# Experts' results weighted on the way out of PSUM and summed by an accumulating scatter

## What is computed

```python
# block one
for e in range(16):
    h = silu(t @ w_e_gate[e]) * (t @ w_e_up[e])
    y = y + comb[:, e:e + 1] * (h @ w_e_down[e])      # comb: routing weight, 0 where not chosen
# block two, rows sorted by expert into blocks of 128
gu = xe @ w_gu[e] + b_gu[e]
act = (clip(gu[:, D_FF:]) + 1) * (x_glu * sigmoid(1.702 * x_glu))   # x_glu = min(gu[:, :D_FF], 7)
yb = act @ w_dn[e] + b_dn[e]
y = zeros((T + 1, D)).at[slot_tok].add(yb * slot_w[:, None])
x = x + gt2 * rmsnorm(y[:T], g_post_ffn)
```

## Time and profile before

| | us |
|---|---|
| median of 3 runs (2850.87 to 2857.93) | 2851.93 |
| profiled execution, its own time | 2854.47 |
| its span, first to last instruction | 2852.7 |
| PE busy | 2502.2 (88%) |
| DVE busy | 2201.2 (77%) |
| ACT busy | 1598.9 (56%) |
| POOL busy | 370.3 (13%) |
| moved by DMA | 731.58 MB, mean 256 GB/s |
| mean granted TensorE clock | 0.934 |

### The profile page before, as it was taken

One profiled execution on the slowest core, in us unless ns is written; L12 is line 12 of the kernel. 1 busy time (PEld: TensorE's weight loads), 2 busy tenths in 40 slices (PEclk: granted clock), 3 DMA queues, 4 the chain that ended last, 5 costly groups with the idle time before them and its releaser, 6 DMA issues. The chain is left out here.

```text
span 2852.7 us, 35466 instructions
## 1 busy us (share of the span) xinstructions
PE 2502.2 (88%) x11972; PEld 2024.1 (71%) x11972; DVE 2201.2 (77%) x2167; ACT 1598.9 (56%) x1491; POOL 370.3 (13%) x297
## 2 busy tenths in 40 slices
PE   7987776999939997778948999999999999999992
PEld 6844665777728895767746777777777777877772
DVE  6787766899854405877557888899988989989985
ACT  3215625777744314555215667677766767667762
POOL 1212001333200000000001111111111111111210
PEclk9998977999969998989958999999999999999996
DMA  8765217999942410021236999999999999999995
GB/s 323 257 214 164 53 55 277 397 400 400 377 143 93 129 53 1 1 89 45 84 126 234 359 363 356 356 360 363 365 365 362 363 362 365 365 356 362 367 353 200
DMA packets 248415, 731.58 MB, mean 256 GB/s; under 512 B 29948, under 2 KB 57867, under 8 KB 246095
## 3 DMA queue, kind: packets, MB, share of 16 engines
q1 hardware_dynamic: 222132, 639.35, 62.2%
q0 software_dynamic: 22240, 80.75, 7.5%
q10 hardware_dynamic: 3968, 10.49, 1.0%
HBM read 692.73 MB, written 39.39 MB: 257 GB/s over the span
## 5 line engine op out<-in xcount | busy, mean ns | idle before, releaser
L49 PE MATMUL psum_all<-sb_ring_r,sb_arena_r 128*128 128x512 f32 (+1 forms) x2400 | 924.7, 385 | 0.0
L157 DVE TENSOR_TENSOR sb_ring_r<-sb_ring,sb_hi_ring 128x2048 fp32r<-128x2048 f32 x285 | 648.7, 2287 | 202.5 <-ACT sb_hi_ring L148 196.1
L148 ACT ACTIVATE sb_hi_ring<-sb_ring 128x2048 fp32r<-128x2048 f32 x285 | 543.3, 1914 | 191.5 <-DMA sb_ring<-in_w_dn_dram 54.1
L157 DVE TENSOR_TENSOR sb_ring_r<-sb_ring,sb_arena_r 128x2048 fp32r<-128x2048 f32 x258 | 581.8, 2284 | 41.2 <-ACT sb_arena_r L148 39.6
L148 ACT ACTIVATE sb_arena_r<-sb_ring 128x2048 fp32r<-128x2048 f32 x258 | 484.5, 1911 | 212.0 <-DMA sb_ring<-in_w_gu_dram 200.3
L48 PE MATMUL psum_all<-sb_hi_ring,sb_arena_r 128*128 128x512 f32 (+1 forms) x1352 | 513.0, 379 | 15.0 <-DVE sb_ring_r L157 5.2
L49 PEld LDWEIGHTS psum_all<-sb_ring_r,sb_arena_r 128*128 128x128 f32 x2400 | 459.1, 191 | 91.8
L50 PE MATMUL psum_all<-sb_hi_ring,sb_arena_r 128*128 128x512 f32 (+1 forms) x1352 | 508.6, 376 | 0.0
L48 PE MATMUL psum_all<-sb_arena_r 128*128 128x512 f32 x1064 | 429.4, 404 | 6.7 <-DVE sb_arena_r L2224 4.7
L50 PE MATMUL psum_all<-sb_arena_r 128*128 128x512 f32 x1080 | 428.0, 396 | 0.0
L48 PEld LDWEIGHTS psum_all<-sb_hi_ring,sb_arena_r 128*128 128x128 f32 x1352 | 259.0, 192 | 68.3 <-DVE sb_ring_r L157 9.5
(11 more groups left out here) (459 smaller groups left out, 3078.5 us busy)
## 6 DMA issues: line engine op xcount, KB each, us to landing
sb_ring<-in_w_gu_dram SPq DMA_DIRECT2D x272, 1024.0 KB, 6.8
sb_ring<-in_w_dn_dram SPq DMA_DIRECT2D x136, 1024.0 KB, 9.3
sb_ring<-in_w_e_gate_dram SPq DMA_DIRECT2D x36, 1024.0 KB, 9.3
sb_ring<-in_w_e_up_dram SPq DMA_DIRECT2D x36, 1024.0 KB, 10.3
sb_ring<-in_w_e_down_dram SPq DMA_DIRECT2D x36, 1024.0 KB, 9.0
sb_ring<-in_w_in_dram SPq DMA_DIRECT2D x27, 1024.0 KB, 5.8
sb_arena<-in_w_ada_dram POOLq DMA_DIRECT2D x32, 512.0 KB, 5.8
sb_ring<-in_w_mod_dram SPq DMA_DIRECT2D x16, 1024.0 KB, 5.2
```

What stands on the lines that cost most here:

```text
L49: eng.matmul(out, a[0], b[1], start=False, stop=False)
L148: act.activation(s.hi[c % len(s.hi)], s.raw[c % len(s.raw)], ACT.Copy).then_inc(s.hi_made, 1)
L157: dve.tensor_tensor(s.lo[c % len(s.lo)], s.raw[c % len(s.raw)], s.hi[c % len(s.hi)].bitcast(F32), ALU.subtract).then_inc(s.lo_made, 1)
```

## The change

One row of y per token. Before the loop y is preset: in block one to zeros, which `route` stores; in block two to routing weights times down biases, which the start of `experts` computes: `route` sums the chosen one-hots times weights into `k.comb` (tokens x experts), TensorE turns it, and eight plain fp32 matmuls with the 32 rows of the down biases give four tiles, which ScalarE copies out of PSUM and SyncE stores. `route` also lists each slot's weight (`item_hot` becomes twice as wide) into `R.share`. `put_y` multiplies by it, and the scatter adds in DRAM. The down projection's bias matmuls, their `select`, and half of the bias table are gone. The combines load one row per token and neither weigh nor add.

```diff
@@ route, SyncE
+            if m.bias is None:
+                sp.wait_ge(s.zeroed, 1)
+                for t in range(TT):
+                    sp.dma_start(m.y[t * P:(t + 1) * P, :], zero).then_inc(R.y_ready, 16)
+            else:
+                b_up, b_down = m.bias
+                sp.dma_start(k.pair[0:m.experts]..., b_down).then_inc(R.bias_landed, 16)
+                sp.wait_ge(s.logits, 1)
+                for half in range(2):
+                    sp.dma_start(k.rows[32 * half:32 * half + m.experts]..., b_up).then_inc(R.bias_landed, 16)
@@ route, POOL
+            if m.bias is None:
+                pool.memset(zero, 0.0).then_inc(s.zeroed, 1)
+            else:
+                pool.wait_ge(s.weighed, 1)
+                for r in range(top):
+                    pool.tensor_tensor(shares[r], chosen[:, r], wide(R.weight[:, :, r], 2, E), ALU.mult)...
+                for r in range(1, top):
+                    pool.tensor_tensor(k.comb[:] if r == top - 1 else shares[0], shares[0], shares[r], ALU.add)...
@@ route, TensorE and VectorE
-                ins = pe.matmul(k.psum[:, 3, 0:NI], slot_hot[:, i, :], item_hot[:, i, :], ...)
+                ins = pe.matmul(k.psum[:, 3, 0:2 * NI], slot_hot[:, i, :], item_hot[:, i, :], ...)
                     dve.tensor_scalar(slot_hot[:, pair, :], k.iota[:], slot_f[:, t, r:r + 1], None, ALU.is_equal)
-                    dve.tensor_scalar(item_hot[:, pair, :], ..., place[:, t, r:r + 1], ...)
+                    dve.tensor_scalar(item_hot[:, pair, 0:NI], ..., place[:, t:t + 1], ...)
+                    dve.tensor_scalar(item_hot[:, pair, NI:2 * NI], ..., R.weight[:, t, r:r + 1], ...)
+            link(dve.tensor_copy(R.share[:, 0:NI], k.psum[:, 3, NI:2 * NI]))
@@ experts, SyncE, after the first item's chunks
+            if biased:
+                for t in range(TT):
+                    sp.wait_ge(s.y_made, t + 1)
+                    sp.dma_start(m.y[t * P:(t + 1) * P, :], first_y[t]).then_inc(R.y_ready, 16)
@@ experts, POOL
                 pool.indirect_dma_start(m.y, bass.IndirectOffsetOnAxis(ap=to_row.bitcast(U32), axis=0),
-                                        ysb.rearrange("p h n -> p (h n)"), None).then_inc(s.y_stored, 16)
+                                        ysb.rearrange("p h n -> p (h n)"), None, compute_op=ALU.add
+                                        ).then_inc(s.y_stored, 16)
             gather(0, True)
             gather(1)
+            pool.wait_ge(R.y_ready, 16 * TT)
@@ experts, TensorE, down()
                         pe.wait_ge(s.y_put, j + 1)
-                        if biased:
-                            pe.wait_ge(s.sel_down, jj)
-                            for hf in range(2):
-                                pe.matmul(k.psum[:, YB + hf, :], sel_down, bias_hl[...], start=True, stop=False)
@@ experts, TensorE, before the first item
+            if biased:
+                for t in range(TT):
+                    ins = pe.transpose(k.psum[0:m.experts, YB, t * P:(t + 1) * P], k.comb[:, t, :], k.ident[:])
+                ins.then_inc(s.comb_turned, 1)
+                pe.wait_ge(s.comb_read, 1)
+                pe.wait_ge(R.bias_landed, 48)
+                for t in range(TT):
+                    if t == 3:
+                        pe.wait_ge(s.y_made, 1)
+                    for hf in range(2):
+                        ins = pe.matmul(k.psum[:, 2 * (t % 3) + hf, :], comb_t[:, t * P:(t + 1) * P],
+                                        b_down[:, 512 * hf:512 * hf + 512], start=True, stop=True)
+                    ins.then_inc(s.y_summed, 1)
             turn_x(0, True)
+            if biased:
+                pe.wait_ge(s.y_made, TT)
@@ experts, ScalarE
                 act.activation(ysb..., k.psum[:, YB:YB + 2, :]...,
-                               ACT.Copy).then_inc(s.y_put, 1)
+                               ACT.Copy, scale=R.share[:, bass.ds(j, 1)]).then_inc(s.y_put, 1)
+            if biased:
+                act.wait_ge(s.comb_turned, 1)
+                act.activation(comb_t, k.psum[0:m.experts, YB, :], ACT.Copy).then_inc(s.comb_read, 1)
             make_hi(act, k, ss, 0)
+            if biased:
+                for t in range(TT):
+                    act.wait_ge(s.y_summed, t + 1)
+                    act.activation(first_y[t], k.psum[:, 2 * (t % 3):2 * (t % 3) + 2, :]..., ACT.Copy).then_inc(s.y_made, 1)
@@ experts, VectorE, before the loop over items
+            if biased:
+                dve.wait_ge(R.y_ready, 16 * TT)
@@ combine_and_normalise and combine_and_store
-            for r in range(2):
-                sp.dma_start(got[:, 2 * t + r, :], y[r * T + t * P:r * T + (t + 1) * P, :])...
+            sp.dma_start(got[:, t, :], y[t * P:(t + 1) * P, :]).then_inc(landed_y[t], 16)
-            act.activation(got[:, 2 * t, :], got[:, 2 * t, :], ACT.Copy, scale=R.weight[:, t, 0:1])...
-            link(dve.scalar_tensor_tensor(out=other, in0=other, scalar=R.weight[:, t, 1:2], in1=mine, ...))
@@ combine_and_store, one transfer, no weighing, no adds
-                ins = dve.scalar_tensor_tensor(out=total[:, t, :], in0=got[:, top * t + r, :],
-                                               scalar=R.weight[:, t, r:r + 1], in1=total[:, t, :], ...)
```

More of the change, by code:

```diff
@@ L1727, in route @@
         pos_i, slot_i, item_i, slot_f, item_f = (take(TT, top) for _ in range(5))
-        place, dest, empty = take(TT, top), take(NI), take(NI)
-        slot_hot, item_hot = take(TT * top, P), take(TT * top, NI)
+        place, dest, empty = take(TT), take(NI), take(NI)
+        shares = [take(TT, E) for _ in range(top)]
+        slot_hot, item_hot = take(TT * top, P), take(TT * top, 2 * NI)
         if G:
@@ L1782, in _ @@
             link(dve.tensor_tensor(logits, psum, wide(bias, 1, TT), ALU.add))
+            dve.sem_inc(s.logits, 1)
             if G:
@@ L1844, in _ @@
             link(dve.tensor_copy(item_f, item_i.bitcast(I32)))
-            for r in range(top):
-                ins = dve.tensor_scalar(place[:, :, r], k.token[:], 1.0 + r * T, None, ALU.add)
-            link(ins)
+            link(dve.tensor_scalar(place, k.token[:], 1.0, None, ALU.add))
             for t in range(TT):
@@ L1925, in experts @@
     if biased:
[L1926 to L1929, removed]
+        bias_hl = take(m.bias[0].shape[1], True)
+        bias_raw = k.rows[0:64].rearrange("p a d -> p (a d)")
+        sel_up = [take(P, True) for _ in range(2)]
+        b_down, comb_t = k.pair[0:m.experts].rearrange("p a d -> p (a d)"), take(T)[0:m.experts]
+        first_y = [prod, h, take(D), take(D)]
     more_hi = [take(CHUNK, True) for _ in range(SLOTS - HI_SLOTS)]
@@ L1958, in _ @@
         def _(sp):
-            if biased:
-                for half in range(2):
-                    for b, raw in zip(m.bias, bias_raw):
-                        sp.dma_start(raw[32 * half:32 * half + b.shape[0], :], b).then_inc(s.bias, 16)
             def up(e, part, c0, per, j):
@@ L2320, in _ @@
                 silu_up(n - 1, PER * n - nB)
-            if biased:
-                select(sel_down, n - 1, s.sel_down)
             done = min(nB, HI_SLOTS)
@@ L2513, in vector @@
         link = chain(dve, s.chain)
-        def add(t):
-            dve.wait_ge(s.weighted, t + 1)
-            for r in range(1, top):
-                dve.wait_ge(landed_y[top * t + r], 16)
-                ins = dve.scalar_tensor_tensor(out=total[:, t, :], in0=got[:, top * t + r, :], scalar=R.weight[:, t, r:r + 1],
-                                               in1=total[:, t, :], op0=ALU.mult, op1=ALU.add)
-                if r < top - 1:
-                    link(ins)
-            ins.then_inc(s.summed, 1)
         def mean(t):
```

135 lines of the change are left out of this document (60 added, 75 removed).

## The result

| | before | after |
|---|---|---|
| median, 6 runs each on one chip | 2853.19 (2848.51 to 2857.93) | 2864.53 (2858.49 to 2866.72) |
| profiled execution, its span | 2852.7 | 2863.7 |
| mean granted TensorE clock | 0.934 | 0.935 |

The changed kernel takes 1.0038 times the time of the one before, 95% interval 1.0026 to 1.0051: 11 us slower, where +31 was forecast. One execution each of x6_sums_moved (7732 us) and x10_no_gate_product_after (7422 us), at a granted clock of 1.00, is left out of their ratios; nothing on record explains them. The scatter is now line L2048, the output copy L2209, the hidden half L2276, the up bias L2101.

A forecast was written before the change was run, and what follows sets the result against it. The prediction took the first loop as DMA-bound with TensorE level, and some 24 of 34 second-loop items as without slack. Its terms, +22 + 25 + 1.3 + 1.3 - 16 - 6.4 + 1.8 + 1 + 1 = +31, gave 2883 us, range 2817 to 2960.

The forecast's parts named there:

- d: Both loops: DMA-engine time of one accumulating scatter above a plain one, taken as 1.3 us, bounds 0 and 3.4.
- +22: First loop: 17 scatters at 1.3 us more each, with no spare DMA time, add 22 us.
- the free add: Rival, both loops: the scatter's addition costs no DMA time, 2818 us in all; chance 0.20.
- the serial trip: Rival, both loops: adding costs a further serial trip, 3.4 us a scatter, 2991 us; chance 0.22 (or between).
- In 24 items: 24 x (1.3 - 0.47) = +20 us.: Second loop: 24 items without slack pay 1.3 us for the scatter, less 0.47 for the removed bias matmuls.
- the forecast's own sign: Both loops: the prediction is wrong if the periods do not grow, or grow by more than 2 us.
- The minus: Second loop: the removed pair of bias matmuls, with its wait, saves 0.47 us per item.
- The plus: Second loop: the scatter's added 1.3 us stands ahead of the first down chunk, in full where no slack is left.
- the second loop swallows it: Rival: the add costs 1.3 us but is covered in the second loop, 2842 us; chance 0.16.
- the 24 waits: Second loop: TensorE waited 24 times, 17.1 us in all, at the first down matmul, just behind the scatter.
- the -15.5 for the biases: Second loop: removing the bias matmuls saves 33 x 0.47 = 15.5 us, a term the rivals booked too.
- -16 + 1.3: Behind block two's last scatter: the one-row combine saves 16 us, the lone scatter costs 1.3 more.

The follow-up runs named there:

- x6_sums_moved: Changed kernel with the bias sums moved behind the chunks of the first item's gate projection; 2860.96 us, ratio to before 1.0026.
- x10_no_gate_product_after: Changed kernel without VectorE's product of gate and sigmoid in block two (wrong activation there); 2853.84 us, ratio to before 1.0004.
- the mean of the six: Mean second-loop stage of six profiles, the changed kernel's among them, that run the same code in its steady state: 1239.4 us (1236.4 to 1243.5).
- x3_no_down_bias: Kernel before without the two down-bias matmuls, their wait and their select, scatter still plain; 2847.9 us, ratio to before 0.9974.
- x2_bias_back: Changed kernel with two bias-like matmuls put back ahead of each block-two down projection, on other operands; 2877.01 us, ratio to before 1.0069.
- x9_no_gate_product: Kernel before without VectorE's product of gate and sigmoid in block two (wrong activation there); 2849.5 us, ratio to before 0.9987.
- x11_after_and_plain: Changed kernel with a second, plain scatter of the same rows into another DRAM tensor behind each accumulating one; 2948.23 us, ratio to before 1.0337.
- x4: Kernel before with every scatter issued a second time, plain, into another DRAM tensor; 2893.45 us, ratio to before 1.0124.
- x7: Changed kernel with block one as before the change, so the change is in block two alone; 2843.54 us, ratio to before 0.9965.
- x5: Changed kernel with its eight bias-sum matmuls over 128 rows, 96 of them zeros; 2854.81 us, ratio to before 1.0005.
- x1: Changed kernel with a plain, overwriting scatter, so a token's rows are not summed; 2836.31 us, ratio to before 0.9929.
- x12: x7 with its eight bias-sum matmuls over 128 rows, 96 of them zeros; 2836.8 us, ratio to before 0.9951.

## Why the prediction was right or wrong

**Right: the price of the add and the first loop.** d = 1.3 was forecast, 1.28 measured there; the software queue's share 19.5% where about 21% was to show it (that had counted 13.6 MB as before, but slower periods hold fewer transfers); the period 19.63 us against the forecast 19.6; the stage +19.7 against +22. The two rivals about d, the free add (0 us) and the serial trip (3.4 us), fall by the same rows.

**Wrong: the second loop.** The step that failed is "In 24 items: 24 x (1.3 - 0.47) = +20 us. In the other 9 that have a scatter ahead I take 0.3 us of slack: 9 x 0.5 = +5. Together +25 us." The measured stage is -2.2, or +0.2 by the mean of the six. By the forecast's own sign, a loop whose period does not grow, this part is wrong: 37.62 before, 37.63 after. The wait at the first down matmul, which was to grow to 1.5 us in nearly all items, is 24.1 us in 31, 0.8 each. Both terms in the bracket were mis-taken. Mean durations of TensorE's segments between 1700 and 2600 us, per item, show it; the nominal chunk is 2.80:

| us per item | last gate chunk, with wait for the hidden half | bias pair | down 1 | down 2 | down 3 | down 4 | period |
|---|---|---|---|---|---|---|---|
| before | 3.64 | 0.54 | 2.80 | 2.80 | 2.83 | 2.82 | 37.66 |
| x3_no_down_bias | 3.47 | - | 2.86 | 2.93 | 3.18 | 2.89 | 37.51 |
| x2_bias_back | 4.20 | 0.54 | 2.80 | 2.80 | 2.80 | 2.80 | 38.09 |
| after | 3.88 | - | 2.87 | 2.80 | 3.03 | 2.90 | 37.64 |
| x9_no_gate_product | 3.53 | 0.54 | 2.80 | 2.80 | 2.82 | 2.81 | 37.52 |
| x10_no_gate_product_after | 3.93 | - | 2.87 | 2.80 | 2.80 | 2.81 | 37.36 |
| x11_after_and_plain | 5.13 | - | 3.67 | 2.80 | 2.90 | 2.85 | 39.65 |

*The minus did not come.* The 0.54 us (taken at 0.47) that TensorE no longer spends on biases come back as waits in the down chunks: from before to x3, +0.06, +0.13, +0.35 and +0.07, 0.61 together. One item of the changed kernel, its scatter in the timeline and then its chain of waits, for the earlier trace rows:

```profile
2236.98 2.90 POOL L2048 DMA_INDIRECT y_dram<-sb_arena  x1 [24.74 <-ACT sb_arena L2209]
...
2242.61 10.37 DMA sb_ring<-in_w_dn_dram
...
2253.09 1.93 ACT sb_hi_ring L148
...
2255.03 2.29 DVE sb_ring_r L157
...
2257.33 0.59 DVE sb_arena_r L2276
...
2258.38 1.83 DVE sb_ring_r L157
...
2260.58 1.22 DVE sb_arena L2281
...
2261.79 1.18 DVE sb_ring_r L157
...
2263.91 0.87 DVE sb_arena L2286
...
2265.05 2.29 DVE sb_ring_r L157
```

Before, the chain went from the hidden half (1.15) to TensorE. Now it stays on VectorE for seven instructions, 10.3 us of work in 12.3 us, splits of weights with the gate's clip (L2281) and its product with the sigmoid (L2286) between them, before it returns to TensorE. Behind the down chunk's landing two paths of nearly equal length run side by side: TensorE's bias pair and four chunks (11.8 us before), and VectorE's work for the same chunks. Shortening TensorE's alone left VectorE's. The forecast had asked of the loop what TensorE and the DMA engines had left, and not VectorE (busy for 994.76 of 1100 us), and had priced the bias pair from TensorE's row alone. VectorE's path was so near that 0.1 us an item (3.2 us in 33) was all that its turn left of the saving, and TensorE's waits of before show almost nothing of it (3.2 us in 900).

*The plus did not come either.* I had taken an item without slack to pass on all of d. With d in place the wait for the hidden half grew by 0.56 an item (x2) or 0.24 (after), not 1.3 to 1.5. The landings point to where the rest went. The scatter's own, before:

```profile
y_dram<-sb_arena POOLq DMA_INDIRECT x29, 8.3
```

It went from 8.3 to 10.6 us, the down chunk's from 9.4 to 9.7, and for the scatter's nobody waits in a hurry. The loop's 362 GB/s against 399 did mean room, though the DMA share stood at 0.99: x4 moved 372 GB/s there. The argument against the rival "the second loop swallows it" was the 24 waits; that rival had the d part nearly right, and its 2842 missed because it too booked the -15.5 for the biases. x11 shows that the room was good for about one scatter's worth: the next 1.3 us arrived in full.

Set against its own twin without the add, each kernel's wait grew by about as much: 0.41 us from x3 to the changed kernel, 0.56 from the kernel before to x2. But in the changed kernel part of this falls where TensorE would have waited for VectorE a little later: down 2 and down 3 are 0.13 and 0.15 shorter than in x3, and the period grew by 0.13 only. This may be why the add costs 14.5 us with the bias pair and next to nothing without it; it is read from the table and was not tested by itself. What holds the shift at 0.4 to 0.6 out of 1.3 to 1.5 us is open. That the transfers share the engines, so that a longer one mostly delays itself, fits the landings but was not tested by itself either.

**The small terms.** Behind the last scatter: forecast -16 + 1.3, measured -13.5. Its chain, for the earlier trace rows:

```profile
2835.76 6.28 DMA y_dram<-sb_arena
...
2842.47 4.60 DMA sb_arena<-y_dram
...
2849.80 1.29 DVE sb_arena L2544
...
2859.18 0.69 DVE sb_x L2548
```

The scatter takes 6.28 us instead of 3.38 when it stands alone: +2.9, where I had put d, 1.3. Beside other traffic d is engine time, alone it is latency, and that is twice as much. The same fits block one's last scatter: from it to the next stage's first matmul 42.9 us before, 38.95 after, so -4.0 against -6.4 + 1.3. Route of block two: from that matmul to the last instruction +7.8 in this profile, +3.6, +4.0 and +4.3 in x7, x5 and x1, against +3.4 worked out; the rest is this profile's own. I had let the loop's start absorb it. It did not, because the bias sums took 14.0 us, the upper bound, where I took 10: from routing's last instruction to the first up matmul 23.0 us (22.2 before, forecast 19 to 23), and to the first scatter 86.0 (86.2 before). With the -4.0 and the +7.8 these make up "between", +3.6 against -3.1. The first stage's +3.4 against +1.8 lies within what it varies from run to run (478.8 to 486.4).

Summed by the measured stages: +3.4 + 19.7 + 3.6 - 2.2 - 13.5 = +11.0, the difference of the spans.

## What to carry to other kernels

An addition in DRAM costs a second transfer's DMA time; put it in the loop whose bytes per second lie below what the same engines reach elsewhere in the trace, and not in the one at that rate (here: block two alone, 0.9965 instead of 1.0038). Before booking a saving on the bound engine, measure the other engine's path between the same two events, since a path 0.1 us shorter hardly shows in the waits; and do not add up two such edits, because the four corners of a square can be 1239, 1236, 1254 and, with both, 1237 to 1239. A lone transfer behind a loop is charged its latency, not its engine time.

## What the runs showed of the hardware

- An accumulating scatter of 128 rows of 4 KB took 2.59 us of the 16 DMA engines against 1.31 plain, 6.28 us alone against 3.38, and POOL spent 2.7 us (median, second loop) on issuing it against 1.75.
- Plain fp32 matmuls over 32 rows kept TensorE busy for 14.0 us and the granted clock stayed at 0.50. The same matmuls over 128 rows, 96 of them multiplied by zeros, had it at 1.00 within their 8.8 us. So padding a short matmul with zero rows can pay: some 6 us here. x12 repeats it, 8.71 against 14.02.
- In x11 waits of up to 2.6 us at the first down matmul were followed by stretches at the lower clock, and the chunk behind took 3.67 us instead of 2.87; with waits of up to 1.6 us (x2) the mean clock of the loop stayed at 1.00.
- A DMA share of 0.99 at 362 GB/s still took in one more transfer of 1.3 us an item for 0.1 us (no bias pair) to 0.45 us (with it); at 1.04 and 399 GB/s, and after the first in the other loop (x11), hardly anything was free: 1.16 and 1.25 us.
